# Gathered expert rows: buffers with waits of their own, experts chosen one group ahead, dense-stretch rows on VectorE, and an end in halves

## The reference

```python
def peer_ffn(hn, w_pq, sub_keys, u_tab, v_tab):
    q = (xt @ w_pq).reshape(T, PEER_HEADS, 2, PEER_D_KEY // 2)
    s = jnp.einsum('thpd,hpkd->thpk', q, sub_keys)
    top_s, top_i = lax.top_k(s, K)                    # K = 16, 128 keys a side
    cand = top_s[:, :, 0, :, None] + top_s[:, :, 1, None, :]
    best_s, best_c = lax.top_k(cand.reshape(T, PEER_HEADS, K * K), K)
    expert = ia * PEER_N_KEYS + ib                    # one of 16384
    gate = jax.nn.softmax(best_s, axis=-1)
    a = jnp.einsum('td,ted->te', xb, u_tab[eb])       # 128 rows of u per token
    hidden = gb * jax.nn.gelu(a)
    return jnp.einsum('te,ted->td', hidden, v_tab[eb])
# x = x + peer_ffn(rmsnorm(x)); out = rmsnorm(x, norm_final)
```

## Time and profile before

| | |
|---|---|
| runs without profile, 3 | 3187.67 to 3189.98, median 3189.12 us |
| profiled execution | 3181.92 us, its span 3180.1 us |
| busy in the span | PE 2767.9, DVE 2060.5, ACT 1153.3, POOL 928.3 us |
| L2342, u rows on DVE, x256 | 587.0 us |
| L2345, v rows on DVE, x87 | 204.6 us |
| L1262, gathers on POOL, x512 | 880.3 us |

### The profile page before, as it was taken

One profiled execution on the slowest core, in us unless ns is written; L12 is line 12 of the kernel. 1 busy time (PEld: TensorE's weight loads), 2 busy tenths in 40 slices (PEclk: granted clock), 3 DMA queues, 4 the chain that ended last, 5 costly groups with the idle time before them and its releaser, 6 DMA issues.

```text
span 3180.1 us, 34785 instructions
## 1 busy us (share of the span) xinstructions
PE 2767.9 (87%) x12256; PEld 2009.7 (63%) x12256; DVE 2060.5 (65%) x2876; ACT 1153.3 (36%) x1984; POOL 928.3 (29%) x558
## 2 busy tenths in 40 slices
PE   8999989999999999999989893667776888668997
PEld 7888778888887888999778791222222444225443
DVE  5587655555564545355545579877777887668766
ACT  5455655555553345345645541000001322007000
POOL 0011000000000000000000007777677677766753
PEclk9999999999999999989999896898888998987999
DMA  6344445555554554443344339999999999999997
GB/s 257 143 159 159 173 147 197 185 191 191 185 190 169 191 190 170 161 167 137 142 146 159 137 134 420 415 420 419 416 409 418 409 408 420 420 420 359 410 405 289
DMA packets 122291, 837.83 MB, mean 263 GB/s; under 512 B 19786, under 2 KB 19802, under 8 KB 21218
## 3 DMA queue, kind: packets, MB, share of 16 engines
q0 software_dynamic: 78240, 520.30, 40.0%
q1 hardware_dynamic: 43776, 313.73, 27.4%
q10 hardware_dynamic: 144, 2.10, 0.2%
HBM read 883.61 MB, written 4.22 MB: 279 GB/s over the span
## 4 chain that ended last, share of the span: by engine, by line
PE 21%; POOL 13%; DVE 7%; DMA 7%; issue 5%; ACT 3%; DVEq 0%; ACTq 0%; POOLq 0%
POOL rows L1262 13%; PE ps L592 10%; PE ps L1174 5%; DMA rows<-peer_v,arena 4%; PE ps L1184 4%; DMA rows<-peer_u,arena 3%; DVE arena L2342 2%; ACT arena L1713 1%; DVE WL L499 1%; PE ps L1165 0%; ACT arena L1716 0%; PE ps L927 0%; DVE arena L206 0%; DVE arena L199 0%; PE ps L953 0%
## 5 line engine op out<-in xcount | busy, mean ns | idle before, releaser
L1184 PE MATMUL ps<-rows,rstd 128*128 128x512 f32 x1352 | 707.7, 679 | 295.1 <-DMA rows<-peer_v,arena 198.9
L499 DVE SCALAR_TENSOR_TENSOR WL<-ring,PA,WH 128x512 fp32r<-128x512 f32 x896 | 631.9, 752 | 476.6 <-ACT WH L482 461.4
L1184 PEld LDWEIGHTS ps<-rows,rstd 128*128 128x128 f32 x1352 | 283.0, 217 | 705.8 <-issue 433.0
L2342 DVE CUSTOM_DVE_ANT_0 arena<-rows,arena 128x2048 f32<-128x2048 f32 x256 | 587.0, 2293 | 200.2 <-DMA rows<-peer_u,arena 176.7
L481 ACT ACTIVATE WH<-ring,PA 128x512 fp32r<-128x512 f32 x448 | 324.0, 723 | 549.1 <-PE ps L592 391.8
L1262 POOL DMA_INDIRECT rows<-peer_v,arena x256 | 452.5, 1768 | 225.6 <-DVE arena L2342 70.2
L1262 POOL DMA_INDIRECT rows<-peer_u,arena x256 | 427.8, 1671 | 227.3 <-DVE WL L499 101.0
L592 PE MATMUL ps<-WH,HH 128*128 128x512 f32 x1120 | 443.0, 396 | 10.6 <-DVE WL L499 8.2
L592 PE MATMUL ps<-WH,HL 128*128 128x512 f32 x1120 | 438.1, 391 | 0.0
L592 PE MATMUL ps<-WL,HH 128*128 128x512 f32 x1120 | 438.0, 391 | 0.0
L592 PE MATMUL ps<-HH,WH 128*128 128x256 f32 x1088 | 314.5, 289 | 23.2 <-DVE WL L499 23.2
(11 more groups left out here) (354 smaller groups left out, 3362.1 us busy)
## 6 DMA issues: line engine op xcount, KB each, us to landing
ring<-stream SPq DMA_DIRECT2D x292, 1024.0 KB, 4.8
rows<-peer_v POOLq DMA_DIRECT2D x24, 1024.0 KB, 15.2
rows<-peer_u,arena POOLq DMA_INDIRECT x256, 17.3
rows<-peer_v,arena POOLq DMA_INDIRECT x256, 16.2
arena<-xT SPq DMA_DIRECT2D x4, 512.0 KB, 8.9
bias_rows<-bias_scratch POOLq DMA_DIRECT2D x1, 2048.0 KB, 12.2
arena<-xT ACTq DMA_DIRECT2D x1, 2048.0 KB, 10.4
arena<-memT POOLq DMA_DIRECT2D x1, 2048.0 KB, 9.1
```

Source lines behind the costliest of these rows:

```text
L499: ins = nc.vector.scalar_tensor_tensor(out=half_tile(WL, u)[:, s], in0=raw_half(u)[:, s], scalar=gain[d], in1=half_tile(WH, u).bitcast(f32 ...
L1184: last = mm(ps[:, 4 * tt + q, :], DIAG[:, k % DIAGS, :], rows[:, n % ROWS, q * CH:(q + 1) * CH], start=n == mine[0], stop=n == mine[-1])
L2342: ins = V.tensor_tensor_reduce(out=JUNK, in0=rows[:, n % ROWS, :], in1=HN[:, tt, :], scale=1.0, scalar=0.0, op0=ALU.mult, op1=ALU.add, acc ...
```

## The change

- **Waits of the buffers.** Gathers 0 to 3 each wait for the split of the tile whose ring slot they overwrite (the fourth from the end up to the last). A table `SLOTS` gives row `n` the buffer `SLOTS[n % 12]`; rows 4 and 5 take the first halves of `HL` and `HH`, free when the last tile but two has been multiplied, rows 6 and 7 the first halves of `WH` and `WL`, free one tile later, rows 8 to 11 the rest, free at the end.
- **Choices.** `choose(0)` stays, `choose(1)` comes after all splits, and `choose(g + 1)` stands at u row 2 of group `g`. Three operations of 512 elements replace six of 256 in it.
- **Rows.** From `m` = 35 on only two v rows go to PE. 24 dense tiles now lie 2.74 v rows apart instead of 2.45, the last with 8 rows behind it (before 13).
- **The end.** The last three rows are shared: columns 0 to 1023 on VectorE, the rest on PE. The second half of the tokens is added, squared, scaled and stored in two column halves. `GROW` now lies in `JUNK` and is loaded when all 16 groups are finished. Some work areas move (`EQ`, `IA_GATE`, `FS` grows to three columns, `IAF` and `IBF` become one tile `IAB`).

The diff, cut to its core (lines that only replace `rows[:, n % ROWS]` by `rows[:, SLOTS[n % ROWS]]` on PE, and the moved work areas, are left out):

```diff
@@ -36,9 +36,11 @@
+HALF = D // 2
...
-EARLY = 4
+EARLY = 2
+SLOTS = [0, 1, 2, 3, 8, 10, 4, 6, 5, 7, 9, 11]
@@ -46,7 +48,7 @@
-DENSE_FROM, DENSE_STEP = 36, 2.45
+DENSE_FROM, TAIL, SHARED = 35, 8, 3
@@ -59,9 +61,7 @@
-    if m < N_LAST - 13:
-        return m % 8 == 0
-    return m % 2 == 0 and m < N_LAST - 2
+    return m in (N_LAST - TAIL + 1, N_LAST - TAIL + 3)
@@ -77,7 +77,7 @@
-    while _d < N_DENSE and _m + 1 >= DENSE_FROM + DENSE_STEP * _d:
+    while _d < N_DENSE and _m + 1 >= DENSE_FROM + _d * (N_LAST - TAIL - DENSE_FROM) // (N_DENSE - 1):
@@ -96,6 +96,9 @@
+N_ROWS = len(ROW_ORDER)
+FIRST_SHARED = N_ROWS - SHARED
+assert LAST_DENSE == N_ROWS - TAIL - 1
@@ -574,12 +577,14 @@
             sp.dma_start(ring[:, s, :], stream[bass.ds(i * RING + s, 1)].rearrange("a p n -> (a p) n")).then_inc(full[s], 16)
-    sp.wait_ge(sem("peer_scores"), 8)
+    sp.wait_ge(sem("hidden"), GROUPS)
     sp.dma_start(GROW, bass.AP(gfin_row.tensor, 0, [[0, P], [1, D]])).then_inc(sem("gfin_in"), 16)
-    for tt in range(TT):
-        sp.wait_ge(sem("final_ready"), tt + 1)
-        sp.dma_start(out[:, tt, :], FIN[:, tt, :]).then_inc(sem("out_written"), 16)
-    sp.wait_ge(sem("out_written"), 16 * TT)
+    sp.wait_ge(sem("final_ready"), 1)
+    sp.dma_start(out[:, 0, :], FIN[:, 0, :]).then_inc(sem("out_written"), 16)
+    for s in range(2):
+        sp.wait_ge(sem("final_ready"), 2 + s)
+        sp.dma_start(out[:, 1, s * HALF:(s + 1) * HALF], FIN[:, 1, s * HALF:(s + 1) * HALF]).then_inc(sem("out_written"), 16)
+    sp.wait_ge(sem("out_written"), 16 * 3)
@@ -1180,9 +1185,10 @@
-        for q in range(4):
-            last = mm(ps[:, 4 * tt + q, :], DIAG[:, k % DIAGS, :], rows[:, n % ROWS, q * CH:(q + 1) * CH],
-                      start=n == mine[0], stop=n == mine[-1])
+        ends = mine[-1:] * 2 + ([N_ROWS - 1] if tt else mine[-1:]) * 2
+        for q in range(2 if n >= FIRST_SHARED else 0, 4):
+            last = mm(ps[:, 4 * tt + q, :], DIAG[:, k % DIAGS, :], rows[:, SLOTS[n % ROWS], q * CH:(q + 1) * CH],
+                      start=n == mine[0], stop=n == ends[q])
@@ -1194,7 +1200,7 @@
-        elif tab == "v" and ROW_DONE[n][0] == "pe":
+        elif tab == "v" and (ROW_DONE[n][0] == "pe" or n >= FIRST_SHARED):
@@ -1246,21 +1252,25 @@
     for n, (tab, g, j) in enumerate(ROW_ORDER):
-        if n == 0:
-            pool.wait_ge(split, 2 * N_TILES)
+        if n < 4:
+            pool.wait_ge(split, 2 * (N_TILES - 3 + n))
         elif n == 4:
+            pool.wait_ge(used, 2 * (N_TILES - 2))
+        elif n == 6:
+            pool.wait_ge(used, 2 * (N_TILES - 1))
+        elif n == 8:
...
         if tab == "dense":
-            pool.dma_start(rows[:, n % ROWS, :], v_tab[g * PEER_KEYS:(g + 1) * PEER_KEYS, :]).then_inc(sem(f"row_in{n % ROWS}"), 16)
+            pool.dma_start(rows[:, SLOTS[n % ROWS], :], v_tab[g * PEER_KEYS:(g + 1) * PEER_KEYS, :]).then_inc(sem(f"row_in{n % ROWS}"), 16)
...
         nc.gpsimd.indirect_dma_start(
-            out=rows[:, n % ROWS, :], out_offset=None, in_=u_tab if tab == "u" else v_tab,
+            out=rows[:, SLOTS[n % ROWS], :], out_offset=None, in_=u_tab if tab == "u" else v_tab,
@@ -1721,9 +1731,9 @@
-    def final_squares(tt):
-        act.wait_ge(sem("sum_ready"), tt + 1)
-        ch.mark(A(FIN[:, tt, :], XN[:, tt, :], ACT.Square, accum_out=FS[:, tt:tt + 1]), "final_squares")
+    def final_squares(n, tt, s):
+        act.wait_ge(sem("sum_ready"), n + 1)
+        ch.mark(A(FIN[:, tt, s], XN[:, tt, s], ACT.Square, accum_out=FS[:, n:n + 1]), "final_squares")
@@ -1736,16 +1746,16 @@
             gate(g + EARLY - 1)
-        if tab == "v" and ROW_DONE[n][0] == "pe":
+        if tab == "v" and (ROW_DONE[n][0] == "pe" or n >= FIRST_SHARED):
...
             ch.mark(A(PO, PO, ACT.Tanh, scale=math.sqrt(2 / math.pi)), "peer_tanh")
-        if n == LAST_DENSE + 4:
-            final_squares(0)
-            root("final0", FS[:, 0:1])
-    final_squares(1)
+    final_squares(0, 0, slice(0, D))
+    root("final0", FS[:, 0:1])
+    final_squares(1, 1, slice(0, HALF))
+    final_squares(2, 1, slice(HALF, D))
@@ -2309,11 +2319,10 @@
-        for part in range(2):
-            ch.link(V.tensor_tensor(EQ, BF[:, part, :].rearrange("p (k a) -> p k a", a=1).to_broadcast([P, 16, 16]),
-                                    i16.rearrange("p (a k) -> p a k", a=1).to_broadcast([P, 16, 16]), ALU.is_equal))
-            ch.link(V.tensor_tensor(EQ, EQ, tif[:, h, part, :].rearrange("p (a k) -> p a k", a=1).to_broadcast([P, 16, 16]), ALU.mult))
-            ch.link(V.tensor_reduce((IAF, IBF)[part][:, tt, es], EQ, X, ALU.add))
+        ch.link(V.tensor_tensor(EQ.rearrange("p b k i -> p (b k) i"), BF.rearrange("p b (k a) -> p (b k) a", a=1).to_broadcast([P, 32, 16]),
+                                i16.rearrange("p (a k) -> p a k", a=1).to_broadcast([P, 32, 16]), ALU.is_equal))
+        ch.link(V.tensor_tensor(EQ, EQ, tif[:, h, :, :].rearrange("p b (a k) -> p b a k", a=1).to_broadcast([P, 2, 16, 16]), ALU.mult))
+        ch.link(V.tensor_reduce(IAB[:, :, tt, es], EQ, X, ALU.add))
@@ -2324,11 +2333,8 @@
     choose(0)
-    W.until(T_PQ + 12)
+    W.until(T_PQ + 16)
     choose(1)
-    W.until(T_PQ + 16)
-    for g in range(2, EARLY):
-        choose(g)
@@ -2339,11 +2345,12 @@
-            ins = V.tensor_tensor_reduce(out=JUNK, in0=rows[:, n % ROWS, :], in1=HN[:, tt, :], scale=1.0, scalar=0.0,
+            ins = V.tensor_tensor_reduce(out=JUNK, in0=rows[:, SLOTS[n % ROWS], :], in1=HN[:, tt, :], scale=1.0, scalar=0.0,
...
-            ins = V.scalar_tensor_tensor(out=XN[:, tt, :], in0=rows[:, n % ROWS, :], scalar=GA[:, tt, at:at + 1],
-                                         in1=XN[:, tt, :], op0=ALU.mult, op1=ALU.add)
+            s = slice(0, HALF if n >= FIRST_SHARED else D)
+            ins = V.scalar_tensor_tensor(out=XN[:, tt, s], in0=rows[:, SLOTS[n % ROWS], s], scalar=GA[:, tt, at:at + 1],
+                                         in1=XN[:, tt, s], op0=ALU.mult, op1=ALU.add)
@@ -2372,12 +2379,12 @@
-    def add_sum(tt, done, read):
+    def add_sum(tt, q0, q1, done, read):
...
-        x = XN[:, tt, :]
-        ch.link(V.tensor_tensor(x, x, ps[:, 4 * tt:4 * tt + 4, :].rearrange("p a b -> p (a b)"), ALU.add))
+        x = XN[:, tt, q0 * CH:q1 * CH]
+        ch.link(V.tensor_tensor(x, x, ps[:, 4 * tt + q0:4 * tt + q1, :].rearrange("p a b -> p (a b)"), ALU.add))
@@ -2398,13 +2405,17 @@
     def last_norm(tt):
-        dve.wait_ge(sem("final_squares"), tt + 1)
+        dve.wait_ge(sem("final_squares"), 1 + 2 * tt)
         fs = FS[:, tt:tt + 1]
+        if tt:
+            ch.link(V.tensor_tensor(fs, fs, FS[:, 2:3], ALU.add))
...
         ch.link(V.reciprocal(fs, fs))
-        V.scalar_tensor_tensor(out=FIN[:, tt, :], in0=XN[:, tt, :], scalar=fs, in1=GROW,
-                               op0=ALU.mult, op1=ALU.mult).then_inc(sem("final_ready"), 1)
+        for s in range(1 + tt):
+            cols = slice(s * HALF, (s + 1) * HALF if tt else D)
+            V.scalar_tensor_tensor(out=FIN[:, tt, cols], in0=XN[:, tt, cols], scalar=fs, in1=GROW[:, cols],
+                                   op0=ALU.mult, op1=ALU.mult).then_inc(sem("final_ready"), 1)
@@ -2412,30 +2423,32 @@
             finish(GROUPS - 1, done)
-            add_sum(0, done, ROW_DONE[ROW_AT["v", PEER_H - 1, PEER_K - 1]][1])
+            add_sum(0, 0, 4, done, ROW_DONE[ROW_AT["v", PEER_H - 1, PEER_K - 1]][1])
...
             ia_gates(*ONE_HOT_AT[n])
-        if n == LAST_DENSE + 3:
-            add_sum(0, done, ROW_DONE[LAST_DENSE][1])
+        if n == LAST_DENSE + 4:
+            add_sum(0, 0, 4, done, ROW_DONE[LAST_DENSE][1])
             dve.sem_inc(sem("sum_ready"), 1)
-        if n == LAST_DENSE + 8:
+        if n == FIRST_SHARED:
...
             last_norm(0)
-        if n == len(ROW_ORDER) - 1:
-            add_sum(1, done, _count["pe"])
+        if n == FIRST_SHARED + 1:
+            add_sum(1, 0, 2, done, _count["pe"])
...
                 finish(g - 1, done)
-            if j == 7 and 0 < g <= GROUPS - EARLY:
+            if j == 2 and 0 < g <= GROUPS - EARLY:
...
     dve.wait_ge(sem("rows_dve"), done)
+    dve.sem_inc(sem("sum_ready"), 1)
+    add_sum(1, 2, 4, done, _count["pe"] + SHARED)
...
```

16 lines of the change are left out of this document (8 added, 8 removed).

## The result

Four runs of the changed kernel took 3164.10 to 3173.34 us, median 3169.66, beside 3189.55 us for the kernel before on the same chip: a ratio of 0.9936 (95% interval 0.992 to 0.9952). That is 19.9 us faster. The forecast was 3165.0 us with a range of 3154 to 3179, and a chance of 0.88 for faster. The profiled execution took 3164.1 us, its span is 3162.3 us; against 3180.1 us that is 17.8 us less.

The account below looks back on a forecast made before the run. The prediction took DMA transfer of gathered rows and dense tiles to bound the expert stage. Terms summed to 24.1 us, taking the profiled 3181.92 to 3157.8; with 7.2 us for the median, 3165.0 us, eight in ten within 3154 to 3179.

Parts of the forecast that it names:

- The rows ahead: Start of the gathers: three gathers leave before the last split, while the DMA has nothing to do; 7.5 us saved.
- The continuous queue: Start of the gathers: the last split ends earlier and the queue is continuous from gather 3 on; 4.0 us saved.
- VectorE's early first row: Start: VectorE reaches its first row at 1905 instead of 1920.75 us; this alone saves nothing, DMA being the bound.
- the shallow queue: From 1905 us on: gathers leave at 2.44 us each, only one to two in flight; 2 us lost (0 to 5).
- The choices: Groups' u rows: choices move from row 7 to row 2, one group ahead; together -0.5 us (-3 to +1).
- Rival D: Expert groups: choices at row 2 drain the queue each time, 18 us; 3183 us, no change; chance 0.06.
- The final gain: Its 1 MB load leaves the full queue and is issued near 2870 us, before the dip; 2.0 us saved (0 to 2.5).
- The dense stretch: Beside the dense tiles: PE no longer holds buffers back, the missing DMA share returns; 1.5 us saved (-6 to +3.5).
- The end: Behind the last landing: 14.9 us to the span's end instead of 26.5; 11.6 us saved (6 to 13).
- A: Start of the gathers: gains nothing, as GpSimd's 2.44 us a gather sets the pace; 3174.5 us, chance 0.13.
- B: End: VectorE arrives some 9 us late, its stock of rows not worked off beside the dense tiles; 3174 us, chance 0.11.
- C: VectorE's rows: each gather between two rows holds VectorE 0.99 us, a row takes 3.4 us; 3205 us, chance 0.04.

Follow-up runs that it names:

- e1: The changed kernel with the old wait, no gather before the last split of the weight tiles: 3178.26 us, 0.997 of the kernel before.
- e9: The changed kernel with the choices at u row 7 and the old wait, no gather before the last split: 3169.15 us, 0.9947 of the kernel before.
- e5: The changed kernel with four groups chosen before the rows and the rest at u row 7, as before the change: 3174.64 us, 0.9961 of the kernel before.
- e2: The changed kernel with the choices back at u row 7, still one group ahead: 3167.11 us, 0.9935 of the kernel before.
- e10: The changed kernel with the choices at u row 7, run a second time: 3166.20 us, 0.9941 of the kernel before.
- e6: The changed kernel with the final gain in its own memory, loaded behind the last scores as before: 3173.84 us, 0.9965 of the kernel before.
- a0: The changed kernel again, unedited: 3170.36 us, 0.9943 of the kernel before.
- b0: The kernel before again, unedited, for a second profile: 3184.28 us in one run.
- e4: The changed kernel with last three rows and second half's sum, squares, norm and store whole, on VectorE alone: 3173.92 us, 0.9953 of the kernel before.

## Why the prediction was right, and where it was not

It was right in sign and range, and nearly in size: 24.1 us forecast, 19.9 in the medians, 17.8 in the pair of profiles, 11.9 to 17.8 over both profiles of the changed kernel against the first of before. On the ruler, without the work ahead of the table load, it is 16.3 and 10.5 us, so part of the nearness in size is luck. The steps:

- **The rows ahead, 7.5 us.** The gathers left at 1875.5, 1881.3 and 1887.9; the forecast said 1877, 1883 and 1889. Their worth is right at gather 30 (7.2 to 7.8 us, e1) and stays where the queue stays full (6.6 to 7.3 us at the last u row, e9). In this kernel 1.0 to 2.9 are left at the last u row (e1).
- **The continuous queue, 4.0.** On the ruler the last split ends at 128.2 us where it was 132.1: 3.9. At gather 3 the kernel before is 3.9 us behind e9 too. The DMA share is 1.01 in 1920 to 1940.
- **VectorE's early first row, "this alone saves nothing, DMA being the bound".** Right as it stands: between the kernel before and e9 VectorE's first row comes 15.3 us earlier, and the distance at gather 30 (6.3 us) is the one at gather 8 (6.4). What the forecast missed is that the rows ahead need it: they fill the twelve buffers sooner, and where VectorE is late GpSimd waits 8.49 us for its first row and 4.4 to 5.1 us are gone (e5 against e2 and e10). The price named with it, -2.0 for the shallow queue, isn't seen: 422 GB/s at one gather per VectorE row, as the earlier trace rows had it.
- **The choices, -0.5 (-3 to +1).** This is the step that failed at the start. At u row 2 they cost 4.3 to 6.9 us against row 7 (e2, e10). "At row 7 it is the same stall" is true of VectorE's 10 us and false of the queue: at row 7 GpSimd has six free buffers to fill while VectorE chooses, at row 2 it had two. Rival D had this mechanism, at 1.2 us in each group. It cost more and came only at the first choices: with a share of 0.86 in 1960 to 1980 and 0.98 in 1980 to 2000 against 1.01 the first takes 3.0 + 0.6 = 3.6 us, and at gather 80, behind the second, the changed kernel is 3.6 to 6.2 us behind e2 and e10, as far as at the last u row. From there on nothing more is lost.
- **The final gain, +2.0.** Right in the queue (2.1 to 2.7 us at gather 30, e6), and lost behind the choices as the rows ahead are: nothing of it is found at the last u row.
- **The dense stretch, +1.5 (-6 to +3.5).** Half of 4 points over 200 us is 4.0 us, not 3.5. From the last u row to the last landing: 296.2 and 297.8 us before, 292.1 and 300.9 after, 295.3 in the mean of ten profiles. That is 1.7 us less, as forecast in size, and less than the scatter. The share rose to 1.00 in 3080 to 3100 from 0.97 and 0.99, but a mean over 16 engines isn't what a landing waits for: behind 3100 the spread of the parts grew with it, from 8.2 and 8.3 us to 13.7 and 15.2. That the time came back there, in the drain, is the reading that fits; no run tests it. GpSimd's waits on the dense tiles fell from 65.0 us only to 50.9, not nearly to nothing. The waits of 2940 to 3150 (total us, times, longest):

```profile
POOL rows L1272 <- PE ps L1179: 43.8, 17, 5.9
DVE XR L2352 <- DMA rows<-peer_v,arena: 39.3, 24, 2.4
PE ps L1179 <- DMA rows<-peer_v: 21.0, 14, 2.2
...
POOL rows L1267 <- PE ps L1179: 7.1, 5, 2.4
```

- **The end, +11.6 (6 to 13).** This term was mis-sized, outside its own range. The place after was forecast to 0.1 us: 14.9 us behind the last landing, 14.8 measured (13.7 in a0). Counted from the last dense tile, as the forecast did, the end was to be at 32.3 us and is at 32.3 (33.4 in a0), and the chain from 3136.78 is the one that was counted out. The place before was wrong. I took the fall of the share at 3153 to 3154 for the last landing. But 0.35 was the drain's beginning; the last part landed at 3161.9, and of before:

```profile
3152.00:3154.00 2.00, 0.35 (x1) 0.30 (x2) 1.64 (x4) 0.99 (x4) 0.00 (x0) 1.00 0.43 180
3154.00:3156.00 2.00, 2.00 (x4) 0.87 (x3) 2.00 (x2) 0.09 (x1) 0.00 (x0) 0.63 0.14 57
3156.00:3158.00 2.00, 2.00 (x4) 0.68 (x2) 2.00 (x1) 0.00 (x0) 0.00 (x0) 0.52 0.76 315
3160.00:3162.00 2.00, 2.00 (x6) 0.90 (x5) 1.90 (x2) 0.00 (x0) 0.00 (x0) 1.00 0.10 41
```

  the share 0.76 is the first half's output, issued at 3155.83, beside the slowest parts of the last gather. So the end was 18.2 us behind the last landing (16.7 in b0), not 26.5, and the gain 3.4 us (3.0 in the second profiles). Measured from the last u row to the end, with the dense stretch in it: 314.5 us before in both profiles, 306.9 to 314.6 after, mean 309.6 over the eight profiles with this end and skipping. 4.9 us, of which e4 gives 4.5 to the halves, where the forecast had 13.1 for the two terms.
- **Not in the sum.** 1.5 to 3.6 us of the profiles' difference lie ahead of the table load, in work that the change doesn't touch.

So the start, the choices and the gain's load, forecast at 11.0 us, brought 8.7 and 10.6 at the last u row. The way there was another. At gather 30 the changed kernel is 13.6 and 13.4 us ahead of the kernel before, and the forecast's gains up to there are 7.5 + 4.0 + 2.0 = 13.5: this mechanism is right, without the 2.0 that was taken off for a shallow queue. Then 3 to 5 us of it are lost by the last u row, where the forecast had 0.5; with the choices at row 7 it becomes 14.9 and 15.6 instead. So a price that didn't come and a loss put too low made each other good in part, which is luck. That 1 to 2 us more are gained with row 7 behind gather 30 no run explains. The term that was mis-sized and not made good is the end.

Rivals: A is refuted by 422 GB/s and by the 7.2 to 7.8 us at gather 30. B is refuted, VectorE waits for landings in 24 places beside the tiles. C is refuted, a VectorE row takes 2.35 us with and without a gather beside it, while the gather takes 2.14 us instead of 0.99. D is refuted in its sum (18 us) and right in its mechanism. The rule of the Trainium skill (SBUF — State Buffer, the rule of the exclusive shared port pair) holds in one direction here: GpSimd pays, and no row shows VectorE paying. The box of that page, which the prediction names beside the rule, speaks of VectorE's two-port modes, and the prediction carried its descriptors over to instructions with two inputs; 422 GB/s at one gather per VectorE row say that here they were written in time.

It stays open why the changed kernel's last stretch differs by 8.8 us between its two executions, where that of the kernel before differs by 1.6.

## What to carry to other kernels

- Work that blocks the engine which frees the buffers costs by what the queue holds when it starts. Put it where many buffers have just come free, not early for its own sake; the place was worth 4 to 7 us here together with rows sent ahead, and 0.6 without them.
- Gains at the start of a queue don't add up by themselves. Follow one numbered transfer through all variants: the place where two kernels draw level is the place where the gain was lost.
- A full mean DMA share says nothing of the slowest of the engines. Look at how far the parts of one transfer end apart before a drain or a dip is priced.
- Find the last landing by the completions, not by where the share falls; and count an end chain on both sides from the last wait for data, which is earlier.

## What the runs showed of the hardware

- The 16 parts of a 1 MB gather with skipped entries end 8 to 15 us apart late in the span, without skipping 9.7 and 10.2 us, of which the first fifteen take 2.5 and 3.7: one part stays 6.6 to 7.2 us behind the others.
- Skipping saves 0.33 to 0.36 us of 2.48 a row.
- Two executions of one kernel reach the table load within 0.1 us of each other (1765.2 and 1765.3; 1768.1 and 1768.0), except the kernel before (1766.7 and 1768.9); kernels that differ only behind it reach it up to 9.4 us apart.
- A gather on GpSimd takes 2.14 us beside a two-input VectorE row of 2048 elements, 0.99 us beside small work.
